# Two transformer blocks on one core: the residual x kept by token instead of by feature, and a rebuilt entry

## The chip, the core and the metric

One Trainium2 chip, one core, no collective. The metric is the device time of one execution in microseconds, median over runs.

## The reference

x is 256 tokens by 1024 features, float32. Two blocks run in sequence:

```python
# block one
h = rms_norm(x, norm_mix_pre)
p = h @ w_in                     # q, k, v, glu, gates
mixed = g_a * (dilated_attention(q, k, v) @ w_attn_out) + g_c * (conv_branch @ conv_pw_w)
x = x + rms_norm(mixed @ w_out, norm_mix_post)
h = rms_norm(x, norm_ffn_pre)
u = causal_depthwise_conv(h @ w_up)
x = x + rms_norm((gelu(u_gate) * u_val) @ w_down, norm_ffn_post)
# block two
x = x + 0.5 * swiglu(rms_norm_2(x, ffn1_norm), w1, w3, w2)
h = rms_norm_2(x, mix_norm)
x = x + (gate_a * rwkv7(h @ w_in) + gate_b * fox(h @ w_in)) @ w_out
x = x + 0.5 * swiglu(rms_norm_2(x, ffn2_norm), w1, w3, w2)
return rms_norm_2(x, final_norm)
```

`rms_norm` divides each token by the root of the mean of its 1024 squares and multiplies by a gain per feature. The squares are summed over features, the gains are per feature.

## The kernel before, in words

All weights stream through three slots of SBUF in chunks of 1 MB (128 x 2048 floats), 172 of them, each loaded by SP's queue once the chunk three before it is split. Splitting makes two fp32r halves of a chunk: `w_hi` by ScalarE (ACT, L1294), `w_lo` by VectorE (DVE, L1551) or, for the first 26 chunks, by GpSimd (POOL, L1244). The activations are split likewise (`X_hi`, `X_lo`, `Y_hi`, `Y_lo`), and each product is three matmuls (`three`, L1918 to L1923).

`by_columns` multiplies 256 output columns of a weight with the whole of X: 16 weight tiles, 3 matmuls of 256 moving columns each, 48 in a chunk. `by_rows` (L1954) takes 256 rows of a weight and adds into all 1024 outputs, again 48 matmuls of 256 columns; its result lies by feature, so x is kept by feature too (`x`, 8 tiles of 128 features by 256 tokens). Only the last feed-forward's down projection is done by tokens: `rows_to_tokens` (L1975) makes the activation the stationary operand and the weight the moving one, 24 matmuls of 512 columns; `x_to_tokens` (L1995) first puts x itself into those banks with 16 fp32 matmuls.

Stages in order, by the index of their first chunk: the entry (chunk 0), the first mixer (glu, qkv, gates, projections, `A_WO` the four chunks of `w_out`, which end at `A_END`), feed-forward 0 (11 rounds of gate, value and down chunk, with a convolution on DVE), feed-forward 1 (to `B0`), the second mixer (to `ffn_at[2]`, its last four chunks from `B_WO` being `w_out_2`), feed-forward 2 and the end. Between two stages lies a boundary:

- The result of the stage lands in four PSUM banks. With a post norm (after `A_END` and feed-forward 0) ACT squares it, PE sums the squares over features with ones (L2009, 4 matmul calls per pair of tiles), ACT takes the root (L1305 loads a table, L1307), DVE makes two diagonals (L1563, L1565), PE spreads them over partitions (L2026), DVE multiplies (L1604) and adds into x (L1609). Without one DVE adds into x directly (L1625).
- ACT makes `X_hi` from x and the gain (L1325), DVE `X_lo` (L1573), and the stage's first chunk is multiplied unnormed as they come.
- For the pre norm ACT squares x (L1300), and after the first chunk PE runs `sum_squares` (L2009, 16 calls, 32 records). The root, the diagonals and the spread follow, the spread in the middle of the second chunk; ACT copies it out as `rstd` (L1316), and every result of the stage is multiplied by it on its way out of PSUM. ACT splits the third chunk between the root and this copy.

The entry: SP loads x (1 MB, one DMA) and chunks 0 to 2. PE turns x by feature (L2074, 16 transposes), DVE copies it out (L1714). ACT's queue issues 16 small loads of parameter rows (L1353); PE turns them at once (L2078), because the first norm's gain is among them. ACT splits chunk 0, then makes `X_hi`. After chunk 0 PE runs `sum_squares`, turns four more groups of parameters (L2095), and makes the table of position biases (L2099), all ahead of chunk 1.

Every order is written out by hand, engine by engine, with counted semaphores. The part of the loop that feeds PE is one `Fori` per feed-forward.

Of the kernel before, what the change touches and what calls it, by code (L numbers as in the profile page):

```python
# [8 lines left out]
F32 = mybir.dt.float32  # L9
# [5 lines left out]
P = 128  # L15
# [73 lines left out]
def block_pair(nc, inp, out, scratch, shifted):  # L89

    ctx = ExitStack()
    with ctx:
# [11 lines left out]
        x = sb("x", [P, NT, T])  # L104
# [3 lines left out]
        eps = sb("eps", [P, 4])  # L108
        rcol, rstd, diag = sb("rcol", [P, 4]), sb("rstd", [P, T]), sb("diag", [P, TT, P])
# [69 lines left out]


# [100 lines left out]
        LAYER_ENDS = (A_WO, A_END, ffn_at[1], B0, ffn_at[2], TOTAL)  # L281
# [21 lines left out]
        x_in = region(0, TT, D)  # L303
        par_in = region(2048, 5, P)

# [4 lines left out]
        final_gain = region(4096, D)  # L310
# [3 lines left out]
        gained = region(6144, 4, 2 * T)  # L314
# [33 lines left out]
        for n in [*range(A_PA), *range(B0, B_RP)]:  # L348
            bank_of[n] = n % 3
            times[n % 3] += 1  # L350
            reads[n] = times[n % 3]

# [68 lines left out]
        def pe_mixer(told, pe, state, by_columns, by_tokens, by_rows, sum_squares, spread):  # L421
            def columns(n, fresh=False, tokens=False, midway=None):
# [36 lines left out]
            columns(B0, fresh=True)  # L459
            sum_squares()  # L460
# [234 lines left out]
            for n in range(B_FP, ffn_at[2]):  # L695
# [4 lines left out]
                else:  # L700
                    r = n - B_WO
                    pe.wait_ge(S["mixed_lo"], 4 + r + 1)
                    by_rows(n, n % RING, 0, X_hi, X_lo, 2 * r, r == 0, r == 3, final=r == 3)


        def act_mixer(told, act, a, split, square, root, spread, state):
# [444 lines left out]
        def _(sp):  # L1151
            told = Count()

            def load(n, slot, parts):

                if n == RING:
                    sp.wait_ge(S["w_lo_first"], 1)
                elif RING < n < BY_POOL + RING:
                    sp.wait_ge(S["w_lo_pool"], n - RING)
# [7 lines left out]
            sp.dma_start(x_in, inp["x"].rearrange("a (t p) d -> p (a t) d", p=P)).then_inc(S["x_landed"], 16)  # L1167
            for n in range(RING):
                load(n, n % RING, chunks[n])
            sp.wait_ge(S["par_cleared"], 1)  # L1170
            for group, row, lo, ap in staged:
                if group > 0:
                    n, c = ap.shape
                    sp.dma_start(par_in[row:row + n, group, lo:lo + c], ap).then_inc(S["rest_landed"], 16)
            sp.dma_start(heads[0:BUCKETS, 0:GROUPS * HPG], inp["rel_bias"]).then_inc(S["rel_landed"], 16)
            gain = inp["final_norm_2"]
            for n in range(RING, TOTAL):
                load(n, n % RING, chunks[n])
                if n == ffn_at[2] + 12:
                    sp.dma_start(final_gain, bass.AP(gain.tensor, gain.offset, [[0, P], [1, D]])).then_inc(  # L1180
                        S["final_gain"], 16)
# [19 lines left out]
        def _(pool):  # L1201
# [19 lines left out]
            g.memset(ones[:], 1.0).then_inc(S["pool_step"], told.one("pool_step"))  # L1221
# [24 lines left out]

# [962 lines left out]
```

## Time and profile before

| what | value |
|---|---|
| median of 3 runs | 1256.07 us (1255.26 to 1256.3) |
| the profiled execution, its own time | 1257.25 us |
| its span, first to last instruction | 1255.5 us |
| mean granted TensorE clock | 0.962 |
| busy: PE, DVE, ACT, POOL | 1197.8, 775.2, 551.0, 154.6 us |
| matmul records on PE | 10503 |
| HBM read, mean rate | 185.70 MB, 150 GB/s |

The span is 1.75 us shorter than that execution's own time, which is 1.18 us above the median. Matmuls overlap in the records, so the step from one start to the next tells the pace, not the duration of one. A granted clock of 1.00 is the full 2.4 GHz, 0.50 is 1.2 GHz.

### The profile page before, as it was taken

The numbers are of one execution on the slowest core, as the hardware profiler recorded it, in microseconds if no ns is written. First come the engines' busy times: TensorE is split into PE (matmuls) and PEld (weight loads), VectorE is DVE, ScalarE is ACT, GpSimd is POOL, SyncE is SP. The second block draws the span as 40 slices with busy tenths as digits, with TensorE's granted clock in tenths as the row PEclk, the third lists the DMA queues.
The fourth block names the chain that finished last, engine by engine and source line by source line (L and its number), as shares of the span: only waits on it lengthen the run. The fifth ranks groups of instructions, "written<-read, shape, count | busy, mean of one in ns | idle before, by whom it ended". The sixth has DMA issues, their size and how long they took to land.

```text
span 1255.5 us, 23871 instructions
## 1 busy us (share of the span) xinstructions
PE 1197.8 (95%) x10503; PEld 1160.5 (92%) x10503; DVE 775.2 (62%) x1057; ACT 551.0 (44%) x613; POOL 154.6 (12%) x113
## 2 busy tenths in 40 slices
PE   6999999989899999989999998999899979999998
PEld 5999999989899999989999997989898879999997
DVE  3588976746587776765554566864266564555554
ACT  4433445473465554453433445523233354444343
POOL 3888770000000000000000000012000000000000
PEclk8999999999799999989999997999999989999999
DMA  6577553345155555526555543332032343565561
GB/s 210 167 233 240 170 168 132 113 146 174 51 184 186 193 175 169 199 65 203 169 169 194 172 151 104 115 103 84 22 101 91 112 134 102 168 210 171 172 199 67
DMA packets 143744, 187.97 MB, mean 150 GB/s; under 512 B 4384, under 2 KB 128857, under 8 KB 143661
## 3 DMA queue, kind: packets, MB, share of 16 engines
q1 hardware_dynamic: 142317, 183.22, 44.5%
q0 software_dynamic: 1104, 3.49, 0.8%
q8 instruction: 63, 1.03, 0.3%
q14 instruction: 20, 0.16, 0.0%
q10 hardware_dynamic: 240, 0.06, 0.0%
HBM read 185.70 MB, written 2.64 MB: 150 GB/s over the span
## 4 chain that ended last, share of the span: by engine, by line
PE 90%; DVE 5%; ACT 3%; issue 1%; ACTq 0%; DMA 0%; POOL 0%; DVEq 0%; POOLq 0%
PE bank L1921 24%; PE bank L1922 24%; PE bank L1923 24%; PE bank L536 2%; PE bank L2009 2%; PE bank L1987 2%; PE bank L1988 2%; PE bank L1989 2%; DVE w_lo L1551 1%; PE bank L596 1%; ACT w_hi L1294 1%; PE bank L2155 1%; DVE bank L1756 1%; PE bank L660 1%; PE bank L662 1%
## 5 line engine op out<-in xcount | busy, mean ns | idle before, releaser
L1921 PE MATMUL bank<-X_hi,w_hi 128*128 128x256 f32 x1968 | 572.3, 291 | 17.2 <-DVE X_lo L1573 11.7
L1922 PE MATMUL bank<-X_lo,w_hi 128*128 128x256 f32 x1968 | 567.3, 288 | 0.0
L1923 PE MATMUL bank<-X_hi,w_lo 128*128 128x256 f32 x1968 | 566.9, 288 | 0.0
L1921 PEld LDWEIGHTS bank<-X_hi,w_hi 128*128 128x128 f32 x1968 | 388.7, 197 | 22.4 <-issue 15.8
L1294 ACT ACTIVATE w_hi<-w_raw 128x2048 fp32r<-128x2048 f32 x172 | 328.5, 1911 | 178.0 <-PE bank L1923 164.8
L1922 PEld LDWEIGHTS bank<-X_lo,w_hi 128*128 128x128 f32 x1968 | 388.8, 198 | 0.4
L1923 PEld LDWEIGHTS bank<-X_hi,w_lo 128*128 128x128 f32 x1968 | 388.4, 197 | 0.0
L1551 DVE TENSOR_TENSOR w_lo<-w_raw,w_hi 128x2048 fp32r<-128x2048 f32 x146 | 333.8, 2287 | 84.1 <-ACT w_hi L1294 83.9
L1654 DVE TENSOR_TENSOR arena<-bank,rstd 128x512 f32<-128x512 f32 x66 | 45.7, 692 | 202.5 <-PE bank L1923 189.8
L1921 PE MATMUL bank<-Y_hi,w_hi 128*128 128x256 f32 x480 | 137.7, 287 | 2.3 <-DVE Y_lo L1103 1.4
L1922 PE MATMUL bank<-Y_lo,w_hi 128*128 128x256 f32 x480 | 136.8, 285 | 0.0
L1923 PE MATMUL bank<-Y_hi,w_lo 128*128 128x256 f32 x480 | 136.7, 285 | 0.0
L1244 POOL TENSOR_TENSOR w_lo<-w_raw,w_hi 128x2048 fp32r<-128x2048 f32 x25 | 116.0, 4647 | 39.3 <-ACT w_hi L1294 39.2
L1921 PEld LDWEIGHTS bank<-Y_hi,w_hi 128*128 128x128 f32 x480 | 93.2, 194 | 3.1 <-DVE Y_lo L1103 1.6
L1756 DVE SCALAR_TENSOR_TENSOR bank<-arena,par,bank 128x256 f32<-128x256 f32 x232 | 93.2, 486 | 0.6
L1922 PEld LDWEIGHTS bank<-Y_lo,w_hi 128*128 128x128 f32 x480 | 93.2, 194 | 0.0
L1923 PEld LDWEIGHTS bank<-Y_hi,w_lo 128*128 128x128 f32 x480 | 93.2, 194 | 0.0
L1275 POOL TENSOR_TENSOR arena<-arena,levels 128x512 f32<-128x512 f32 x10 | 12.7, 1279 | 622.8 <-DVE arena L997 589.2
L1366 ACT ACTIVATE arena<-arena,par 128x256 f32<-128x256 f32 x44 | 24.2, 599 | 71.8 <-DVE arena L1654 71.8
L1375 ACT ACTIVATE arena<-arena 128x512 f32<-128x512 f32 x22 | 14.0, 635 | 88.3 <-DVE arena L1654 88.3
L1589 DVE TENSOR_TENSOR arena<-bank,rstd 128x512 f32<-128x512 f32 x43 | 29.7, 690 | 36.4 <-PE bank L1923 32.4
L1389 ACT ACTIVATE Y_hi<-arena 128x512 fp32r<-128x512 f32 x33 | 20.9, 633 | 44.0 <-DVE arena L1679 25.0
(283 smaller groups left out, 1193.4 us busy)
## 6 DMA issues: line engine op xcount, KB each, us to landing
w_raw<-in_ffn_w_dram SPq DMA_DIRECT2D x66, 1024.0 KB, 5.3
w_raw<-in_w_in_dram SPq DMA_DIRECT2D x54, 1024.0 KB, 5.1
w_raw<-in_w_up_dram SPq DMA_DIRECT2D x22, 1024.0 KB, 5.1
w_raw<-in_w_down_dram SPq DMA_DIRECT2D x11, 1024.0 KB, 4.9
w_raw<-in_w_out_dram SPq DMA_DIRECT2D x8, 1024.0 KB, 4.9
w_raw<-in_conv_pw_w_dram SPq DMA_DIRECT2D x4, 1024.0 KB, 4.8
w_raw<-in_w_attn_out_dram SPq DMA_DIRECT2D x2, 1024.0 KB, 5.0
w_raw<-in_rwkv_proj_dram SPq DMA_DIRECT2D x2, 1024.0 KB, 5.0
```

The lines of the kernel that those rows point to most:

```text
L536: mm = pe.matmul(head(bank[b], h, slice(i * CHUNK, (i + 1) * CHUNK)), left(f, i, h), right(f, i, h), start=True, stop=True)
L1244: g.tensor_tensor(w_lo[n % RING][:, :], raw[n % RING][:, :], w_hi[n % RING][:, :].bitcast(F32), ALU.subtract).then_inc(S["w_lo_pool"], tol ...
L1294: a.activation(w_hi[slot][:, :], raw[slot][:, :], ACT.Copy).then_inc(S["w_hi"], told.one("w_hi"))
L1551: v.tensor_tensor(w_lo[slot][:, :], raw[slot][:, :], w_hi[slot][:, :].bitcast(F32), ALU.subtract).then_inc(S["w_lo"], told.one("w_lo"))
L1589: v.tensor_tensor(dst, pairs(b), over(rstd[:], 2), ALU.mult).then_inc(S[f"bank{b}_read"], 1)
L1654: v.tensor_tensor(u_t[:, side].rearrange("p (m t) -> p m t", m=2), pairs(2 * (i % 2) + side), over(rstd[:], 2), ALU.mult).then_inc(S[name] ...
L1756: v.scalar_tensor_tensor(out=conv[:, t, :] if k == CONV_W - 1 else part, in0=src, scalar=w, in1=part, op0=ALU.mult, op1=ALU.add).then_inc( ...
L1921: pe.matmul(o, wh, xh, start=start, stop=False, skip_group_check=True)
L1922: pe.matmul(o, wh, xl, start=False, stop=False, skip_group_check=True)
L1923: return pe.matmul(o, wl, xh, start=False, stop=stop, skip_group_check=True)
L1987: pe.matmul(o, yh, wh, start=False, stop=False, skip_group_check=True)
L1988: pe.matmul(o, yl, wh, start=False, stop=False, skip_group_check=True)
```

## The change

x lies by token (`x`, two tiles of 128 tokens by 1024 features) from the load to the end. Every down and output projection (`A_WO` to `A_END`, feed-forwards 0 and 1, `B_WO` to `ffn_at[2]`: 30 chunks) goes through `rows_to_tokens`. At each boundary PE turns x into PSUM, 16 transposes, and ACT and DVE make `X_hi` and `X_lo` from there. A token's squares are summed by ACT itself, along the row (`accum_out`), for the post norms and the pre norms; `sum_squares` and `x_to_tokens` go. Gains of post norms are loaded spread over partitions (three DMAs of 512 KB on SP's queue, where there was one). In the entry x and chunk 0 are loaded and split in halves, the first gain is loaded alone and first, ten parameter loads stay on ACT's queue and the rest go to SP's, and all other parameters are turned behind chunk 1 instead of behind chunk 0. Where a stage has no post norm (`B0`, `ffn_at[2]`), the last chunk does the low half of the features first, and PE turns that half two products before the chunk's end, the other half in the middle of the next chunk; with a post norm PE turns all of x after the last chunk, eight transposes for each token tile. `X_hi` is read from PSUM, where a bank's second tile waits for the first one's `X_lo`. The residual of the last feed-forward is added by DVE at the end.

Cut to its core:

```diff
-        x = sb("x", [P, NT, T])
+        x = sb("x", [P, TT, D])
+        HALF_FIRST = (B0, ffn_at[2])
+        TOKEN_ENDS = (A_END, ffn_at[1], B0, ffn_at[2], TOTAL)
 # SP
-            sp.dma_start(x_in, inp["x"]...)
-            for n in range(RING):
+            for h in range(2):
+                sp.dma_start(x[:, :, c], inp["x"]...[:, :, c]).then_inc(S[f"x_landed{h}"], 16)
+            for h in range(2):
+                sp.dma_start(first[:, 4 * h:4 * h + 4, :], chunks[0]...)
+            for n in range(1, RING):
                 load(n, n % RING, chunks[n])
-            for group, row, lo, ap in staged:
-                if group > 0:
+            for group, row, lo, ap in staged[1 + ON_ACT:]:
+            gains = {A_WO: ..., ffn_at[0] + 12: ..., ffn_at[2] + 12: ...}
 # ACT
+            def root_mean(t, halves, root, signal):
+                for h, (source, ready, count) in enumerate(halves):
+                    act.wait_ge(S[ready], count)
+                    a.activation(sq[:, h, :], source, ACT.Square, accum_out=half if h == 0 else whole)
+                    if h == 0:
+                        a.activation(mean, half, ACT.Identity, bias=eps[:, 0:1], scale=1.0 / D)
+                a.activation(root, whole, ACT.Sqrt, bias=mean, scale=1.0 / D)
+            def x_scaled(gain, ends, ahead):
+                for f in range(NT):
+                    high_part(f, gain, ends)
+                for t in range(TT):
+                    token_root(t, ...)
+                split(ahead)
+                spread()
+            act.dma_start(gain_in, inp["norm_mix_pre"]...)
+            for group, row, lo, ap in staged[1:1 + ON_ACT]:
+                act.dma_start(par_in...)
+            root_table()
+            for f in range(NT):
+                if f == 4: first_split(0, "w_hi_first")
+                if f == 6: first_split(1, "w_hi")
+                high_part(f, first_gain, 0)
+            split(1)
+            for t in range(TT): token_root(t, ...)
+            split(2)
+            spread()
 # DVE
+            def post_norm(last, next_gain):
+                for t in range(TT):
+                    for h in range(2):
+                        v.tensor_tensor(gained[:, t, c], bank[4 + 2 * t + h][:, :], token_gain[:, c], ALU.mult)
+                    v.reciprocal(...)
+                    for h in range(2):
+                        v.scalar_tensor_tensor(out=x[:, t, c], in0=gained[:, t, c], scalar=..., in1=x[:, t, c])
+                for f in range(NT): low_part(f, next_gain, last)
+            def residual(last, scale, next_gain, base=4):
+                residual_tile(0, 0); residual_tile(1, 0); low_part(0); low_part(1)
+                residual_tile(0, 1); low_part(2); low_part(3); residual_tile(1, 1)
+                for f in range(4, NT): low_part(f)
 # PE
-                    by_rows(at + 4, ..., 4, Y_hi, Y_lo, ...)
+                    rows_to_tokens(at + 4, ..., (Y_hi, Y_lo), 2 * parity, first and i == 0)
+                    if ends in HALF_FIRST and at == 5:
+                        turn_early_half(ends)
-                sum_squares()
-                x_to_tokens()
+            turn_by_tokens(A_END)
             feed(0)
-                if n == 0:
+                if n == 1:
                     pe.wait_ge(S["constants"], 2)
...
```

## Rows read from the trace of the kernel before

**Rows 1.** the page: busy time of TensorE, and the chain that ended last, by engine
```profile
PE 1197.8 (95%) x10503; PEld 1160.5 (92%) x10503; DVE 775.2 (62%) x1057; ACT 551.0 (44%) x613; POOL 154.6 (12%) x113
...
PE 90%; DVE 5%; ACT 3%; issue 1%; ACTq 0%; DMA 0%; POOL 0%; DVEq 0%; POOLq 0%
```

**Rows 2.** PE's waits over the whole run (total, times, longest, us)
```profile
PE bank L1921 <- DVE X_lo L1573: 11.7, 5, 3.6
...
PE bank L466 <- ACT arena L720: 4.8, 1, 4.8
```

**Rows 3.** PE timeline, one chunk by 256 columns and one by 512
```profile
1097.31 0.28 PE L1921 MATMUL bank<-X_hi,w_hi 128*128 128x256 f32 x1
...
1103.07 0.40 PE L1987 MATMUL bank<-w_hi,Y_hi 128*128 128x512 f32 x1
...
1108.54 0.28 PE L1921 MATMUL bank<-X_hi,w_hi 128*128 128x256 f32 x1
```

**Rows 4.** busy time by stretch: loop, one boundary in four, two later ones
```profile
400.00:417.28 17.28, 17.28 (x147) 17.28 (x146) 12.43 (x16) 8.85 (x10) 0.00 (x0) 1.00 0.56 184
...
319.90:327.30 7.40, 2.46 (x21) 2.19 (x19) 4.88 (x11) 3.74 (x8) 0.00 (x0) 0.78 0.15 61
...
334.70:338.70 4.00, 4.00 (x34) 4.00 (x33) 0.00 (x0) 0.00 (x0) 0.00 (x0) 0.87 0.01 4
...
338.70:344.50 5.80, 5.80 (x28) 5.80 (x29) 0.84 (x4) 2.56 (x3) 0.00 (x0) 0.50 0.00 0
...
344.50:347.60 3.10, 3.10 (x28) 3.10 (x28) 3.10 (x4) 2.50 (x3) 0.00 (x0) 1.00 0.00 0
...
745.40:751.50 6.10, 6.10 (x53) 6.10 (x54) 4.52 (x10) 2.57 (x3) 0.00 (x0) 1.00 0.01 3
...
1071.00:1074.50 3.50, 3.50 (x35) 3.50 (x33) 3.02 (x3) 2.94 (x2) 0.00 (x0) 1.00 0.78 238
```

**Rows 5.** the critical chain in time order: six transposes
```profile
216.81 0.67 PE bank L2131 x6
```

**Rows 6.** DVE timeline, end of the first mixer
```profile
314.43 2.29 DVE L1551 TENSOR_TENSOR w_lo<-w_raw,w_hi 128x2048 fp32r<-128x2048 f32 x1 [3.47 <-ACT w_hi L1294]
...
326.71 0.88 DVE L1573 SCALAR_TENSOR_TENSOR X_lo<-x,par,X_hi 128x256 fp32r<-128x256 f32 x2
```

**Rows 7.** DVE timeline, start of the second mixer
```profile
733.97 1.41 DVE L1625 SCALAR_TENSOR_TENSOR x<-bank,x 128x512 f32<-128x512 f32 x2
...
747.95 2.29 DVE L1551 TENSOR_TENSOR w_lo<-w_raw,w_hi 128x2048 fp32r<-128x2048 f32 x1 [0.80 <-ACT w_hi L1294]
...
750.16 0.68 DVE L1589 TENSOR_TENSOR arena<-bank,rstd 128x512 f32<-128x512 f32 x1
```

**Rows 8.** PE timeline, entry
```profile
5.99 3.65 PE L2074 MATMUL bank<-ident,arena 128*128 128x128 f32 x16 [5.99 <-DMA arena<-in_x_dram]
...
12.34 0.33 PE L2078 MATMUL bank<-ident,arena 128*128 128x128 f32 x1 [2.70 <-DMA arena<-in_rwkv_k_a_dram]
...
15.94 0.55 PE L1921 MATMUL bank<-X_hi,w_hi 128*128 128x256 f32 x1 [3.26 <-DVE X_lo L1573]
...
23.63 3.73 PE L2009 MATMUL bank<-ones,sq 128*128 128x1 f32 x32
...
30.90 0.58 PE L1921 MATMUL bank<-X_hi,w_hi 128*128 128x256 f32 x1
```

**Rows 9.** ACT timeline, entry
```profile
7.34 0.32 ACTq L1353 DMA_DIRECT2D arena<-in_rwkv_k_a_dram  x1
...
9.44 1.91 ACT L1294 ACTIVATE w_hi<-w_raw 128x2048 fp32r<-128x2048 f32 x1 [0.47 <-DMA w_raw<-in_w_in_dram]
```

**Rows 10.** SP timeline, entry
```profile
15.42 43.19 SPq L1165 DMA_DIRECT2D w_raw<-in_w_in_dram  x7
```

**Rows 11.** ACT timeline, last token tile
```profile
1250.01 0.60 ACT L1526 ACTIVATE sq<-bank 128x512 f32<-128x512 f32 x1 [0.34 <-PE bank L1989]
...
1250.73 0.30 ACT L1530 ACTIVATE small<-small 128x1 f32<-128x1 f32 x1
```

More of the change, by code:

```diff
@@ L351, in block_pair, with turned_place @@
             reads[n] = times[n % 3]
+        def turned_place(f, ends):
+            early, late = (2, 3), (4, 5)
+            if ends == B0:
+                early, late = (1, 3), (4, 6)
+            if ends in (0, ffn_at[2]):
+                early, late = (4, 5), (6, 7)
+            c = f % 4 // 2 * T
+            return bank[(early, late)[f // 4][f % 2]][:, c:c + T]
         def all_read(before):
@@ L702, in pe_mixer, with act_mixer @@
                     pe.wait_ge(S["mixed_lo"], 4 + r + 1)
-                    by_rows(n, n % RING, 0, X_hi, X_lo, 2 * r, r == 0, r == 3, final=r == 3)
-        def act_mixer(told, act, a, split, square, root, spread, state):
+                    rows_to_tokens(n, n % RING, (X_hi, X_lo), 2 * r, r == 0, ffn_at[2] if r == 3 else None, base=0)
+        def act_mixer(told, act, a, split, spread, state):
             def copies(ready, count, dst, b, name):
@@ L1952, in by_tokens, with by_rows @@
                 mm.then_inc(S["chunk_used"], told.one("chunk_used"))
[L1954 removed]
+            def by_rows(n, slot, first_bank, hi, lo, k0, first, last, final=False):
                 split_ready(n)
@@ L1984, in rows_to_tokens @@
                     c = k * D + 512 * h
-                    yh, yl = (y[:, k0 + k, t * P:(t + 1) * P] for y in (Y_hi, Y_lo))
+                    yh, yl = (y[:, k0 + k, t * P:(t + 1) * P] for y in (hi, lo))
                     wh, wl = (w[slot][:, c:c + 512] for w in (w_hi, w_lo))
-                    pe.matmul(o, yh, wh, start=False, stop=False, skip_group_check=True)
+                    last = ends is not None and k == 1
+                    pe.matmul(o, yh, wh, start=first and k == 0, stop=False, skip_group_check=True)
@@ L2015, in sum_squares @@
-            def sum_squares():
-                for p in range(4):
-                    sum_pair(p)
+                    mm = pe.matmul(o, yh, wl, start=False, stop=last, skip_group_check=True)
+                    if last and at < 7:
+                        mm.then_inc(S["tile_summed"], told.one("tile_summed"))
+                    if ends in HALF_FIRST and at == 5:
+                        turn_early_half(ends)
+                mm.then_inc(S["chunk_used"], told.one("chunk_used"))
+                if ends is not None:
+                    state["ends"] = ends
```

467 lines of the change are left out of this document (236 added, 231 removed).

## The prediction

> **What bounds the kernel now.** I read the page first. PE is busy for 95% of the span, and it carries 90% of the chain that ended last [rows 1]. So what counts is PE's own work and the few places where it waits. PE's waits add up to little: the largest is five waits for `X_lo`, 11.7 us in all, which are the boundaries between stages, then 4.8 us for the second mixer's first activations [rows 2]. In the loop PE has no gap: 17.28 us for a gate, a value and a down chunk, with DVE busy for 12.43 and ACT for 8.85 [rows 4]. The rest of the loss is seen only by stretches: at a boundary PE counts as busy while it runs small products, or runs at a granted clock of 0.50 [rows 4].
>
> **The down chunks.** A chunk by 256 columns runs from 1097.31 to 1103.07: 48 matmuls, 5.76 us, 120 ns each. The chunk by 512 columns runs from 1103.07 to 1108.54: 24 matmuls, 5.47 us, 228 ns each [rows 3]. Both carry the same 12,288 columns; half as many instructions save 0.29 us. 30 chunks change form. Four of them are the last of a stage and are counted in the boundaries below, so **26 x 0.29 = 7.5 us**. The loop's period falls from 17.28 to 16.99, still above DVE's 12.43 and ACT's 8.85, so all of it is on the path. The Trainium skill (TensorE: Matmul & The Clock Gate, "Back-to-back issue gap") gives a gap of N/2.4 + 2.5 ns, by which the saving of a chunk would be an estimated 24 x 2.5 ns = 0.06 us and this term 1.6 us; the trace disagrees with it in this stream, with 13 ns over the columns' time at 256 and 14 at 512.
>
> **The boundary after the first mixer (`A_END`).** Now: the last chunk starts at 312.2 (PE timeline, 5.76 us and three sums before 319.9). From 319.9 to 327.3 PE mostly waits; the first chunk takes 7.4 us because the clock is low at first; the sums take 4.0; the second chunk takes 5.8 at clock 0.50 and then 3.1 at full clock, to 347.6 [rows 4]. After, from the same start: token tiles end at 313.8, 315.1, 316.5 and 317.8 (6 x 228 ns each). ACT loads its table under the chunk. A square with its accumulator read and the next step takes 0.72, a root 0.30 [rows 11], so ACT has both roots by about 319.9. DVE is the later one: its split ends at 316.7 [rows 6], and then come four products by the gain, two reciprocals and four additions, 0.70 each by the nearest row of that size [rows 7] and 0.15. x's third tile is added at 322.1. PE turns it (16 transposes cost 16 x 0.11 [rows 5] at full clock, twice that at half, of which only two stand ahead of the first `X_hi`), ACT and DVE take 0.45 each [rows 6], and the first chunk starts at **323.8 instead of 327.3**. It still has a gap of 6 us before it, so I leave it 7.4 us. Then the second chunk starts at once, with 48 x 0.12 + 0.4 for the spread = 6.1 us, as in the second mixer's boundary, where no low clock is seen [rows 4]. It ends at 337.4 instead of 347.6: **10.1 us saved**.
>
> What must be ready for the third chunk: ACT ends the last `X_hi` at 326.5, the two roots cost 4 x 0.72 + 4 x 0.30 = 4.1, so 330.6; diagonals 331.4; the spread is due at 333.4, `rstd` 334.4, DVE reads a bank (0.7) and splits (2.29 [rows 6]): 337.3. That is level with PE's 337.4; its cover is gone, and anything later here is time.
>
> **Behind feed-forward 0** the same pattern stands 209 us later, with a last chunk from 521.5 and a first chunk of 7.9 us. DVE is free at 525.7, so by the same steps the first chunk starts at 532.9, the third at 547.0 instead of 556.6: **9.6 us saved**.
>
> **The boundary at `B0`** has no post norm, and no idle to win. Now DVE ends its split at 733.97 and adds two pairs in 1.41 [rows 7]; the last chunk runs from 729.6 to 735.3, the sums from 742.0 to 745.4, the second chunk to 751.5 [rows 4]. After: PE comes to the early transposes at 733.7 and must wait until 735.4 for those two additions; 0.9 for 8 transposes, 1.4 for the rest of the chunk, 1.4 for the first two tiles of the next: 739.1; wait for the last addition until 739.6; 0.9 of transposes; 4.4 for the rest: 744.9. That is only 0.5 earlier than 745.4. What decides is ACT's chain: last `X_hi` at 742.4, roots 4.1, so 746.5 instead of 745.9, then the split of the third chunk, DVE's split (747.95 now) and the read of the bank at 750.16 [rows 7], from which the 4.8 us wait of [rows 2] hangs. **0.5 us lost**, and all that PE gained is waited away.
>
> **The boundary at `ffn_at[2]`** is the same 316.2 us later, but now the second chunk has the low clock and `x_to_tokens` takes 3.5 us to 1074.5 [rows 4]. After: the second chunk runs from 1061.1 to 1067.3; roots at 1062.7, ACT's split to 1064.6, `rstd` 1065.0, bank read 1065.7, split 1067.9. The third chunk starts at 1068.0: **6.5 us saved**.
>
> **The entry.** Now: x landed at 5.99, transposes to 9.6, parameters at 12.34 (the last of 16 issues leaves ACT's queue at 7.66 [rows 9]), chunk 0 starts at 15.94, sums at 23.63, chunk 1 at 30.90, chunk 2 at 38.5 (end of chunk 1) [rows 8]. After: the first half of x lands 1.3 to 1.7 earlier (1 MB takes 3.45, from 5.99 to 9.44 [rows 8, 9]); it is turned at half clock as before, 0.228 each, from 4.7, all of it by 8.4. ACT's eleven issues end at 5.1, its table is loaded by 6.6 with the gain copied; four `X_hi` in turn with DVE to 8.4; half a chunk split to 9.4 (half of 1.91 [rows 9]), its low half on DVE to 10.6. Chunk 0 starts at **10.7 instead of 15.9** and takes 7.7 as now. The second half of chunk 0 lands at 9.44 as now [rows 9] and is split in time (12.8, needed at 15). Chunk 1 starts at 18.4 (its low part is ready at 16.5), takes 6.1, then the parameters take 3.0 (3.5 now, at half clock): chunk 2 at 27.5 instead of 38.5, **11.0 us saved**. ACT's roots end at 18.3, diagonals 19.1, the spread is due at 20.6; POOL has chunk 2 at 24.9. SP's queue takes two halves and five more small loads; it comes to chunk 3 at 15.42 now [rows 10] and some 2 us later then, landed five later, needed at 33. All covered. The first gain takes at most the 5.0 of the last parameter, 7.34 to 12.34 [rows 8, 9]; landing by 5.8 it is still ahead of ACT's 6.6. The two added loads of 512 KB stand in the loop, where DMA's share is 0.56 [rows 4]: no cost.
>
> **The end.** DVE's four additions of 0.70 come between PE and ACT; two of them do not fit beside 1.37 per tile together with the products by the gain: **1.4 us lost** (0.7 if they fitted).
>
> **Sum:** 7.5 + 10.1 + 9.6 - 0.5 + 6.5 + 11.0 - 1.4 = 42.8 us. 1257.25 - 42.8 = 1214.45 for the profiled execution; the median lies 1.2 lower: **1213.3 us**.
>
> **The rivals.**
> - *The clock (0.15).* The transposes and the stalls of 1.7 us could let the clock fall where it now stays up: chunk 2 of the entry behind 3.0 us of parameters, and the chunks at `ffn_at[2]`. A fall cost 5.8 us at 0.50 where 2.7 fewer would do [rows 4]; twice that and 1 us at two others is 6 to 7: 1220. Against it: 3.4 us of sums at 742 did not lower it. The Trainium skill (TensorE: Matmul & The Clock Gate, "PE-mode transpose") says that transposes do not count as busy for the clock; it would give this time. No run here shows it yet: the entry's transposes ran at half clock, from a cold start.
> - *The new chain (0.2).* Roots, spread, bank read and split end later than I have them and gate the third chunk at each of four places by about 2 us: 1221. For it: there is no slack left in three of them. ACT now does eight serial steps where it had four squares.
> - *The gap between the two forms is not there in the loop (0.05).* 7.5 us less: 1221.
> - *Faster still (0.1).* The clock is up for the first chunks, or the first gain and x come sooner: 3 + 3 + 2 less: 1205.
> - *The entry doesn't deliver (0.06).* Small loads queue behind x and chunk 0, or ACT's issues take longer: half of 11.0 is lost: 1219.
> - *Slower (0.02).* The down chunk's operands come late in the loop: ACT and DVE work for `f_lo` is in series, and with the shorter period PE waits in every round. It decides only if each of 22 rounds waits over 2.1 us (46 us in all); then 1259. DVE's 4.85 free microseconds of 17.28 speak against it.
>
> **How the numbers follow.** Forecast 0.42, rivals as given. From 1204 (faster still) to 1225 (two of the lesser ones together) lies 0.8; I leave out the slow end. A measurement tells this kernel from no change at about 0.2%, 2.5 us; all cases but the last lie far beyond: faster 0.96, same 0.02, slower 0.02.
>
> **What would show it.** No L2009 rows; 720 fewer records of main matmuls; the down chunks at 228 ns; chunk 0 at about 10.7 and chunk 2 at 27.5; at both post norms a gap of some 6 us before the first chunk with small waits; at `B0` two waits of 1.7 and 0.5 inside the chunks and the 4.8 us wait grown by about 1; at the end the last square 0.7 later behind the last matmul. I am wrong if a third chunk waits for `w_lo`, if a clock of 0.50 stands in the second chunks, or if the loop's period is not 17.0.

## The result and the profile after

The changed kernel takes **1211.9 us** (median of 4 runs, 1211.0 to 1214.9), the kernel before 1255.7 (1254.9 to 1256.3): a ratio of **0.9656, interval 0.9638 to 0.9674**. The forecast was 1213.3, in a range from 1204 to 1225. The profiled execution took 1212.24 us with a span of 1210.5, against a span of 1255.5 before: 45.0 us to explain, where the working had 42.8.

The page of the changed kernel, the lines of busy time and of the chain that answer to [rows 1]:

```profile
PE 1155.8 (95%) x9584; PEld 1086.6 (90%) x9584; DVE 770.4 (64%) x1042; ACT 557.2 (46%) x660; POOL 149.9 (12%) x112
...
PE 87%; DVE 7%; ACT 4%; issue 2%; DMA 0%; ACTq 0%; DVEq 0%
```

PE has the same share in a shorter span: what went was time in which it counted as busy (one-column products, half clock, more instructions), as the stretches of [rows 4] had hinted. PE's waits, to set beside [rows 2] (total, times, longest, us; L735 is the line that was L720, and L2042 turns x):

```profile
PE bank L481 <- ACT arena L735: 5.6, 1, 5.6
PE bank L2042 <- DVE x L1660: 4.9, 4, 1.4
PE bank L2224 <- ACT arena L1529: 4.5, 4, 3.6
PE bank L2042 <- DVE x L1676: 3.5, 4, 1.5
PE bank L2097 <- DVE X_lo L1159: 3.5, 1, 3.5
```

The five waits for `X_lo` at the stage boundaries are gone. In their place stand eight short ones for x itself, 4.9 and 3.5 us; the wait behind `B0` is the largest now, 5.6 where it was 4.8.

The down chunk by 512 columns, in the PE timeline of the loop of feed-forward 0 (start, duration of one), as the second chunk of [rows 3]:

```profile
337.54 0.40 PE L2097 MATMUL bank<-w_hi,Y_hi 128*128 128x512 f32 x1
...
343.00 0.28 PE L1987 MATMUL bank<-X_hi,w_hi 128*128 128x256 f32 x1
...
354.52 0.40 PE L2097 MATMUL bank<-w_hi,Y_hi 128*128 128x512 f32 x1
```

It takes 5.46 us, and the loop's period is 354.52 - 337.54 = 16.98, as forecast (17.28 before).

The entry, in the PE timeline, beside [rows 8]:

```profile
2.38 0.24 PE L2146 MATMUL bank<-ident,arena 8*128 8x8 f32 x1 [2.38 <-DMA arena<-in_norm_mix_pre_dram]
4.97 3.37 PE L2042 MATMUL bank<-ident,x 128*128 128x128 f32 x16 [2.35 <-DMA x<-in_x_dram]
11.06 0.36 PE L1987 MATMUL bank<-X_hi,w_hi 128*128 128x256 f32 x1 [2.71 <-issue]
...
24.59 0.27 PE L2163 MATMUL bank<-ident,arena 128*128 128x128 f32 x1
...
25.22 1.45 PE L2168 MATMUL bank<-arena 32*4 32x256 f32 x6
26.61 0.39 PE L1987 MATMUL bank<-X_hi,w_hi 128*128 128x256 f32 x1
```

Chunk 0 starts at 11.06 (15.94 before), chunk 2 at 26.61 (38.48 before, the end of chunk 1).

Stretches of the changed kernel (us, busy time and instructions of PE, PE's weight loads, DVE, ACT and POOL, then the granted clock, 1.00 being the level of 2.4 GHz and 0.50 that of 1.2 GHz; a value between is a mixture):

```profile
281.10:283.50 2.40, 0.09 (x2) 0.05 (x1) 2.27 (x5) 1.30 (x3) 0.00 (x0) 1.00 0.88 291
283.50:288.00 4.50, 4.50 (x13) 3.53 (x14) 3.39 (x3) 1.76 (x1) 0.00 (x0) 0.62 0.22 78
306.70:312.80 6.10, 3.34 (x18) 1.99 (x18) 5.46 (x11) 3.16 (x12) 0.00 (x0) 0.91 0.51 172
312.80:315.20 2.40, 2.40 (x12) 2.40 (x12) 1.98 (x6) 2.12 (x6) 0.00 (x0) 0.52 0.00 0
315.20:325.70 10.50, 10.50 (x90) 10.50 (x89) 4.21 (x7) 8.30 (x18) 0.00 (x0) 1.00 0.00 0
...
718.20:723.80 5.60, 5.60 (x17) 4.19 (x17) 3.79 (x4) 3.20 (x5) 0.00 (x0) 0.50 0.08 15
724.00:728.20 4.20, 4.20 (x21) 4.20 (x22) 1.37 (x3) 3.20 (x5) 0.00 (x0) 0.51 0.64 222
```

The boundary at `A_END`: a gap of 6.1 us with two turns in it, 2.4 us of the first chunk at half clock, and then 10.5 us at full clock through the rest of the first and all of the second chunk, where before stood 5.8 us at 0.50 [rows 4]. Each stretch behind a long wait of PE (from 283.5, 312.8 and 718.2) shows a low clock.

**Where the 45.0 us came from**, each piece taken between the same two starts of chunks on PE in both traces (the third chunk of a stage is the end of a boundary and the start of what follows):

| piece | before | after | gain | forecast |
|---|---|---|---|---|
| entry, to the start of chunk 2 | 38.48 | 26.61 | 11.9 | 11.0 |
| first mixer, to `A_END`'s last chunk | 273.7 | 274.9 | -1.2 | 0.9 |
| boundary at `A_END` | 35.3 | 24.4 | 10.9 | 10.1 |
| loop of feed-forward 0 | 173.9 | 171.2 | 2.7 | 2.9 |
| boundary behind feed-forward 0 | 35.2 | 23.8 | 11.4 | 9.6 |
| loop of feed-forward 1 | 173.0 | 170.0 | 3.0 | 2.9 |
| `B0`, to the end of the wait for ACT | 27.2 | 27.2 | 0.0 | -0.5 |
| second mixer | 289.1 | 287.4 | 1.7 | 0.9 |
| boundary at `ffn_at[2]` | 28.7 | 21.7 | 7.1 | 6.5 |
| the end | | | -2.3 | -1.4 |

### The profile page after: what moved, and what is told of

The parts are those of the page before. It is cut to its first block, busy times and chain, and to the rows that moved or that the text cites. A ratio compares the mean times of both kernels' runs of the same rounds, so it can differ in the third digit from the quotient of the medians.

```text
span 1210.5 us, 22075 instructions
## 1 busy us (share of the span) xinstructions
PE 1155.8 (95%) x9584; PEld 1086.6 (90%) x9584; DVE 770.4 (64%) x1042; ACT 557.2 (46%) x660; POOL 149.9 (12%) x112
## 4 chain that ended last, share of the span: by engine, by line
PE 87%; DVE 7%; ACT 4%; issue 2%; DMA 0%; ACTq 0%; DVEq 0%
PE bank L1987 20%; PE bank L1988 20%; PE bank L1989 19%; PE bank L2097 5%; PE bank L2098 5%; PE bank L2099 5%; PE bank L551 2%; DVE w_lo L1602 2%; ACT w_hi L1316 1%; PE bank L611 1%; PE bank L2042 1%; PE bank L2224 1%; DVE bank L1819 1%; PE bank L675 1%; PE bank L677 1%
## 5 line engine op out<-in xcount | busy, mean ns | idle before, releaser
L1987 PE MATMUL bank<-X_hi,w_hi 128*128 128x256 f32 x1840 | 529.2, 288 | 2.8 <-issue 2.7
L1988 PE MATMUL bank<-X_lo,w_hi 128*128 128x256 f32 x1840 | 525.5, 286 | 0.0
L1989 PE MATMUL bank<-X_hi,w_lo 128*128 128x256 f32 x1840 | 525.2, 285 | 0.0
L1988 PEld LDWEIGHTS bank<-X_lo,w_hi 128*128 128x128 f32 x1840 | 358.1, 195 | 1.2
L2097 PE MATMUL bank<-w_hi,Y_hi 128*128 128x512 f32 x264 | 103.3, 391 | 1.2 <-DVE Y_lo L1742 1.2
L2098 PE MATMUL bank<-w_hi,Y_lo 128*128 128x512 f32 x264 | 103.1, 390 | 0.0
L2099 PE MATMUL bank<-w_lo,Y_hi 128*128 128x512 f32 x264 | 102.7, 389 | 0.0
L2097 PEld LDWEIGHTS bank<-w_hi,Y_hi 128*128 128x128 f32 x264 | 49.7, 188 | 11.1 <-DVE Y_lo L1742 1.6
L2099 PEld LDWEIGHTS bank<-w_lo,Y_hi 128*128 128x128 f32 x264 | 49.6, 188 | 10.6
L2098 PEld LDWEIGHTS bank<-w_hi,Y_lo 128*128 128x128 f32 x264 | 49.7, 188 | 9.1
```

Source lines behind the costliest of these rows:

```text
L1987: pe.matmul(o, wh, xh, start=start, stop=False, skip_group_check=True)
L1988: pe.matmul(o, wh, xl, start=False, stop=False, skip_group_check=True)
L1989: return pe.matmul(o, wl, xh, start=False, stop=stop, skip_group_check=True)
L2097: pe.matmul(o, yh, wh, start=first and k == 0, stop=False, skip_group_check=True)
L2098: pe.matmul(o, yl, wh, start=False, stop=False, skip_group_check=True)
L2099: mm = pe.matmul(o, yh, wl, start=False, stop=last, skip_group_check=True)
```

## The experiments

Theory: the gain is PE time, in three kinds. Half as many matmuls in the down chunks; one-column products, the turn back to tokens and idle time taken out of the boundaries; and, as a consequence that I had counted only in part, less time at half clock. Rivals: the 512-column form gains nothing where other engines hide it; the third chunk of a stage waits for the row scale anyway, so that what stood ahead of it cost little; the entry's gain has one source alone. Medians in different series differ by up to 3.5 us for one kernel (1254.3 and 1257.8 for the kernel before), so each edit is read at its place in the trace first and in the median second.

### Half width

```diff
-                    pe.matmul(o, yl, wh, start=False, stop=False, skip_group_check=True)
+                    for q in range(2):
+                        c2 = slice(256 * q, 256 * q + 256)
...
+                        pe.matmul(o[:, c2], yl, wh[:, c2], start=False, stop=False, skip_group_check=True)
...
```

> Edit: every 512-column matmul of the down, A_WO and B_WO chunks is issued as two of 256 columns, nothing else. Theory (a matmul costs its columns plus some 13 ns): 41 chunks x 0.29 us = 11.9 us more than the changed kernel's 1211.9, so 1223.8, and each such chunk again near 5.76 us. Rival (a back-to-back matmul costs its columns plus 2.5 ns): 41 x 0.06 = 2.5 us, so 1214.4. Rival (the 256-column form is hidden behind the other engines in the loops): under 4 us, so below 1216.

Measured 1223.5 us (1220.7 to 1225.6), ratio 0.9728 (0.9702 to 0.9754); the span is 1221.7, 11.2 longer than the changed kernel's. The same place in its PE timeline:

```profile
337.23 0.28 PE L2099 MATMUL bank<-w_hi,Y_hi 128*128 128x256 f32 x1
...
343.11 0.28 PE L1988 MATMUL bank<-X_lo,w_hi 128*128 128x256 f32 x1
```

49 matmuls in 5.88 us, 120 ns each, against 24 in 5.46 above. The width of the instruction is worth 0.3 us a chunk. For the kernel it is worth 9 us by the ratios (0.9728 - 0.9656, of 1256) and 11.2 by the spans, where 11.9 was expected; both rivals (2.5, and under 4) fall, so little of it is hidden. A matmul of this stream costs 13 to 14 ns over its columns' time at either width. The Trainium skill (TensorE: Matmul & The Clock Gate, "Back-to-back issue gap") has 2.5 ns there for a matmul by itself, from which an estimated 1214.4 would have followed; for a stream of weight loads and matmuls the same section has about 131 ns at 512 columns, against the 228 ns seen here. The measurement decides against both.

### Sums back, and turns in their place

```diff
                 mm.then_inc(S["chunk_used"], told.one("chunk_used"))
                 if fresh:
                     state["xg"] += 1
+                    for i in range(16):
+                        pe.matmul(bank[3][:, 256 + i % 2:257 + i % 2], ident[:], ident[:, 0:1], start=True, stop=True)
```

The second kernel has `for i in range(32): pe.transpose(bank[3][:, 256:384], ident[:], ident[:])` there instead.

> Edit: behind the first chunk of each of the five fed stages 16 fp32 matmuls of one column, as the kernel before had for its sums of squares, with no wait of their own and no reader. Theory (their time stood in the way in four of five places, and the clock fell behind them): some 3.5 us at the entry, A_END, ffn_at[1] and ffn_at[2] = 14, little at B0, where 5.6 us of idle time follow, and up to 2.9 us more in each place where the granted clock falls to half behind them: 1226 to 1235. Rival (the third chunk waits for the row scale anyway, so they are absorbed): 0 to 5 us more, 1212 to 1217.

> Edit: in the same five places 32 fp32 transposes of 128x128 instead (0.11 us each at full clock, 3.5 us together). Theory from the traces (transposes at full length hold the clock, as 16 of them did between two chunks at B0): 4 x 3.5 = 14 us more, 1226, and a granted clock of 1.00 in the chunk behind them at B0 and ffn_at[2]. Rival (transposes do not count as work for the clock, which the Trainium skill's page TensorE: Matmul & The Clock Gate states under PE-mode transpose; what follows from it is that the chunk behind them is at half clock for some microseconds): 2.9 us more in up to five places, 1229 to 1240, and a granted clock near 0.5 there.

With the sums 1236.8 us (1234.9 to 1239.3), ratio 0.9830 (0.9808 to 0.9853), span 27.0 longer; with the turns 1228.0 (1223.1 to 1232.0), ratio 0.9752 (0.9719 to 0.9786), span 19.8 longer. (By the ratios it is 21.9 and 12.1 us; the profiled execution of the turns was the slowest of its four.) Both groups last 3.5 us. Stretches of the kernel with the sums: the sums of feed-forward 1's boundary, then what follows:

```profile
525.70:529.30 3.60, 3.60 (x35) 3.60 (x33) 0.00 (x0) 0.83 (x1) 0.00 (x0) 0.99 0.00 0
529.30:532.60 3.30, 3.30 (x17) 3.30 (x17) 0.00 (x0) 0.00 (x0) 0.00 (x0) 0.50 0.00 0
```

The same two of the kernel with the turns:

```profile
521.60:525.10 3.50, 3.50 (x35) 3.50 (x33) 0.65 (x3) 2.15 (x3) 0.00 (x0) 1.00 0.00 0
525.10:529.00 3.90, 3.90 (x35) 3.90 (x34) 0.58 (x1) 0.38 (x1) 0.00 (x0) 1.00 0.00 0
```

Of the five places, the clock fell behind the sums in three (entry, feed-forward 1, `ffn_at[2]`), behind the turns in none; in the kernel before it fell behind the sums in four of five, which is the low second chunk of [rows 4]. Some 37 matmuls ran slow behind the sums, at 0.09 us more each: about half of the 7.2 us between the two spans. A good part of the rest stands in chunks ahead of the sums (the first chunks of the entry and of feed-forward 1 had 26 and 19 slow matmuls in the one trace, 16 and 4 in the other), and the same chunks differ as much between two executions of one kernel (26 and 19 in `after_again`, 15 and 5 in the first execution). So the rival that I gave 0.15, that the new transposes lower the clock, is not borne out. The rule beside it, in the Trainium skill (TensorE: Matmul & The Clock Gate, "PE-mode transpose"), was that a transpose doesn't count as busy for the clock; these fp32 turns, which the trace lists as matmuls of 107 ns, held 1.00 for 3.5 us and in the 4 us behind. Whether they use the mode that the page means, no run here shows.

The price at the place: with the turns the third chunk starts 3.5 us later at the entry, `A_END`, feed-forward 1 and `ffn_at[2]`, the full length, so there the row scale doesn't gate it; behind `B0` only 1.2, because the wait for ACT falls from 5.6 to 3.5. That leaves 19.8 - 4 x 3.5 - 1.2 = 4.6 us, and they stand in the second mixer, whose code is the same. I come back to them.

### The entry, part by part

```diff
 entry_whole:
-            for h in range(2):
-                c = slice(512 * h, 512 * (h + 1))
-                sp.dma_start(x[:, :, c], inp["x"].rearrange("a (t p) d -> p (a t) d", p=P)[:, :, c]).then_inc(
-                    S[f"x_landed{h}"], 16)
+            sp.dma_start(x[:, :, :], inp["x"].rearrange("a (t p) d -> p (a t) d", p=P)).then_inc(S["x_landed0"], 16)
...
 params_early:
-                if n == 1:
+                if n == 0:
                     pe.wait_ge(S["constants"], 2)
...
 gain_last:
-            act.dma_start(gain_in, inp["norm_mix_pre"][0].rearrange("(r c) -> r c", c=P)).then_inc(S["par_landed"], 16)
             act.wait_ge(S["par_cleared"], 1)
             for group, row, lo, ap in staged[1:1 + ON_ACT]:
...
+            act.dma_start(gain_in, inp["norm_mix_pre"][0].rearrange("(r c) -> r c", c=P)).then_inc(S["par_landed"], 16)
```

> Edit: x and the first chunk are loaded in one transfer each instead of in halves; the instructions behind them are the same. Theory (the halves let transposes and splits start while the second half is under way, a part of the entry's 11.9 us): the first chunk starts 1 to 2 us later, 1213 to 1214. Rival (the entry is set by the chain of splits, not by landing): within 0.4 us of 1211.9. Rival (two transfers less on the queue help): down to 1211.

> Edit: the parameters are turned behind the first chunk again (as before the change), and copied by DVE behind its first bank; the rest of the entry stays changed. Theory (what matters of this part is only that the last parameter lands near 18.3 us, when the first chunk ends): PE waits under 1 us behind the first chunk and the third chunk starts 0 to 1.5 us later than 26.6 us. Rival (behind the first chunk the eleven small products let the clock fall, as in the kernel before): the second chunk runs at half clock for a while, 2 to 3 us in all. Rival (the position is worth the whole 3.7 us that it took before): 3 us or more.

> Edit: the transfer of the first norm weight is issued behind the ten other parameter transfers of ACT's queue instead of ahead of them. Theory (the entry hangs on x, turned at 4.97 us, and on the ACT table load to 6.6 us; the weight is needed from then on): it is issued near 5.0 us, lands near 7 us, and the first chunk starts 0.5 to 1.5 us later than 11.06 us. Rival (the weight alone is the part that the entry's gain comes from): 3 us or more. Rival (it is hidden behind the first splits): under 0.3 us.

`entry_whole`, 1215.6 us (1215.2 to 1216.4), ratio 0.9669 (0.9649 to 0.9689). Its PE timeline:

```profile
6.17 3.68 PE L2035 MATMUL bank<-ident,x 128*128 128x128 f32 x16 [3.56 <-DMA x<-in_x_dram]
12.04 0.55 PE L1980 MATMUL bank<-X_hi,w_hi 128*128 128x256 f32 x1 [2.19 <-issue]
```

x comes 1.2 us later and chunk 0 0.98 later; with 27 slow matmuls behind it instead of 15 the third chunk starts at 28.81, 2.2 later. The halves are worth 1 us, the low end of the theory; the rest is clock, which `after_again` also has, with its halves (26 slow matmuls).

`params_early`, 1215.5 us (1213.1 to 1218.0), ratio 0.9678 (0.9650 to 0.9707). Its PE timeline behind chunk 0, and the stretch of chunk 1:

```profile
20.24 0.30 PE L2163 MATMUL bank<-ident,arena 128*128 128x128 f32 x1 [1.81 <-DMA arena<-in_conv_dw_w_dram]
20.38 0.60 PE L2165 MATMUL bank<-ident,arena 128*128 128x128 f32 x4
20.91 2.22 PE L2168 MATMUL bank<-arena 32*4 32x256 f32 x6
```

```profile
23.00:27.10 4.10, 4.10 (x20) 4.04 (x20) 0.00 (x0) 0.00 (x0) 2.15 (x1) 0.50 0.43 127
```

Here I was wrong by the size: the last parameter lands at 20.24, not 18.3, so PE waits 1.81; turns and products take 2.8 us instead of 2.0; and the second chunk, 17 of its matmuls at half clock, takes 8.6 instead of 6.2. All that follows starts 5.0 us later. Two of the rivals together are right: having the parameters behind the second chunk is worth 5 us, some 3 of it clock.

`gain_last`, 1217.5 us (1215.8 to 1218.2), ratio 0.9690 (0.9666 to 0.9714). Its issues on ACT's queue, then its PE timeline:

```profile
5.61 0.32 ACTq L1395 DMA_DIRECT2D arena<-in_norm_mix_pre_dram  x1
5.96 1.28 ACT L1354 ACT_TABLE_LOAD   x1 [5.96 <-issue]
```

```profile
10.88 0.24 PE L2146 MATMUL bank<-ident,arena 8*128 8x8 f32 x1 [10.88 <-DMA arena<-in_norm_mix_pre_dram]
11.06 3.67 PE L2042 MATMUL bank<-ident,x 128*128 128x128 f32 x16
16.93 0.55 PE L1987 MATMUL bank<-X_hi,w_hi 128*128 128x256 f32 x1 [2.20 <-issue]
```

I expected 0.5 to 1.5 us and got 5.9: the first chunk starts at 16.93. The 4 KB are issued at 5.61 and landed at 10.88, 5.3 us, behind x and the first megabytes of weights; in the changed kernel they are the first issue of the queue, at 0.81, and have landed by 2.38, in at most 1.6 us. What makes it so dear is PE's order: the gain's own transpose (L2146) stands ahead of those of x (L2042), so x, there since 4.75 and 6.45, is turned only from 11.06, and ACT, its table loaded at 7.24, waits 4.82 us for it. Of the three parts tried, this one delays the third chunk most: 5.9 us, against 5.0 and 2.2. Whether x turned first would have hidden it, no run shows.

### The orders of ACT and DVE around B0

```diff
 squares_early:
                 for f in range(NT):
                     high_part(f, gain, ends)
+                    if f == 3 and ends in HALF_FIRST:
+                        for t in range(TT):
+                            half_mean(t, first + t + 1)
...
 update_first:
                 residual_tile(last, scale, 0, 0, base)
                 residual_tile(last, scale, 1, 0, base)
+                split(last + 1)
                 low_part(0, next_gain, last)
```

(In `update_first` the split is taken out ahead of the stage's end in exchange.)

> Edit: at B0 and ffn_at[2] ACT squares the two early halves of x between the fourth and the fifth high part, where it waits 2.2 us for late transposes, instead of behind the eighth. Theory (at B0 the chain late high parts, four squares, root, split, scale, bank read sets the 5.58 us that PE waits for ACT L735; two squares and a mean less stand in it): the wait shrinks by 1.5 to 2 us, nothing at ffn_at[2]: 1.5 to 2 us less in all. Rival (that wait is set by the bank reads of DVE and its split, so it moves little): under 0.5 us. Rival (the squares delay the fifth high part and with it the first chunk): 0.5 us more.

> Edit: at B0 and ffn_at[2] DVE adds the two early tiles to x ahead of its last split, not behind it, so that PE's transposes in the last chunk don't wait 1.51 us. Theory: 1.5 us less at ffn_at[2], and 1.5 us less at B0 since the high parts and roots all come earlier: 3 us in all. Rival (the split then delays the low parts, so that the first chunk waits as much): 0 to 1 us in all. Rival (B0's gain vanishes in the wait for ACT L735): 1.5 us.

`squares_early`, 1216.2 us (1214.1 to 1217.8), ratio 0.9679 (0.9652 to 0.9705). In its waits of PE:

```profile
PE bank L481 <- ACT arena L735: 3.6, 1, 3.6
```

5.6 became 3.6, so ACT's serial roots do set that wait: the chain that I named for `B0` is shown. The median shows nothing of it, though: the second mixer's stretch behind it (to the end of PE's wait for DVE L1066) takes 181.8 us, where it took 178.8, and up to PE's wait for `X_lo` at `B_WO` it takes 273.0, where it took 265.7.

`update_first`, 1213.1 us (1210.8 to 1216.3), ratio 0.9667 (0.9641 to 0.9694). DVE's timeline in the last chunk ahead of `B0`:

```profile
690.59 0.69 DVE L1676 SCALAR_TENSOR_TENSOR x<-bank,x 128x512 f32<-128x512 f32 x1 [1.33 <-PE bank L2101]
691.95 0.69 DVE L1676 SCALAR_TENSOR_TENSOR x<-bank,x 128x512 f32<-128x512 f32 x1 [0.67 <-PE bank L2101]
692.55 2.28 DVE L1602 TENSOR_TENSOR w_lo<-w_raw,w_hi 128x2048 fp32r<-128x2048 f32 x1
```

Both tiles are added before the split, and PE's two waits of 1.51 us are gone. Counted from the third chunk of feed-forward 1, the wait for ACT ends 1.3 us earlier (195.96 instead of 197.22 us behind it), and `ffn_at[2]`'s third chunk starts 1.3 earlier, counted from PE's wait for `X_lo` at `B_WO`: 2.6 where 3 was expected. (From the third chunk of feed-forward 0 the first of the two looks like 2.1, but 0.9 of that is the boundary behind feed-forward 0, where the clock fell for no matmul in this trace and for five in the other.) The span is only 1.4 shorter, since the mixer between took 2.9 back.

### The same kernel again, and PE kept busy

```diff
+            def keep_busy(n, b, count):
+
+                split_ready(n)
+                for _ in range(count):
+                    pe.matmul(bank[b][:, :], w_hi[n % RING][:, 0:P], w_hi[n % RING][:, 0:512], start=True, stop=True)
...
             columns(B0 + 1, midway=spread)
+            keep_busy(B0 + 2, 6, 22)
...
+                        pe.wait_ge(S["attn_gated"], 4)
+                        keep_busy(n, 7, 9)
                     pe.wait_ge(S["mixed_lo"], r + 1)
```

and the like at the other places (at the entry ten fp32 matmuls of 128 columns). The tail's edit in `order_all` is DVE's order alone:

```diff
+            residual_tile(TOTAL, 0.5, 0, 0)
+            residual_tile(TOTAL, 0.5, 0, 1)
             for t in range(TT):
                 for h in range(2):
-                    residual_tile(TOTAL, 0.5, t, h)
+                    if t == 1 and h == 0:
+                        residual_tile(TOTAL, 0.5, 1, 1)
...
+                if t == 0:
+                    residual_tile(TOTAL, 0.5, 1, 0)
```

> Edit: none, the changed kernel once more, beside the three below. It gives the spread of its stages between executions. Theory (the second mixer, from the end of its wait for ACT L735 to the wait for DVE L1066, took 178.8 to 182.1 us in nine kernels that are the same there, by where the clock falls): total 1211 to 1216, that stretch anywhere from 178.8 to 182.1. Rival (the longer stretches come from the edits made in the experiments): 178.8 again.

> Edit: three orders at once. The two early tiles ahead of DVE's last split (update_first), the early squares between the fourth and fifth high part (squares_early), and in the tail the additions of the last tiles ahead of the gains and of the reciprocal of the tile before. Theory: 2.1 at B0 and 1.3 at ffn_at[2] as measured alone, 2.0 more at B0 for the squares, about 1 us in the tail from the last matmul to the end (7.8 us in the changed kernel): 6 us less, less what falls of the clock take back in the second mixer. Rival (the mixer takes it back by the clock): the total is within 2 us of after_again though the three places are shorter.

> Edit: only matmuls that nobody reads, in places where PE waits: behind the turns at the entry (10 fp32 of 128 columns), at A_WO (9 of 512 columns), in the three gaps of each of A_END and ffn_at[1] (5 or 2, 6 and 2), ahead of the wait for lora_act behind B0 (22) and at B_WO (7). Theory (the granted clock falls behind an idle PE): the slow matmuls behind these gaps (15, 9, 9, 5, 19 and 8 in the changed kernel) go to full pace: 48 x 0.12 + 17 x 0.18 = 8.8 us less; where some gaps are overfilled, 5 to 9 us less. Rival (the clock falls there whatever PE does in the gap): no slow matmul less, and 0 to 3 us more from overfilled gaps. Rival (the falls move to other places): within 2 us of after_again.

> Edit: order_all and keep_warm together, with 14 instead of 22 matmuls behind B0, where the gap is shorter. Theory: the gains of both add, 10 to 14 us less than after_again, 1198 to 1203. Rival (the clock takes it back): 1206 to 1210.

All four beside the same runs of the kernel before:

| kernel | median (range), us | ratio (interval) |
|---|---|---|
| `after_again` | 1214.7 (1211.2 to 1217.7) | 0.9654 (0.9637 to 0.9671) |
| `order_all` | 1207.1 (1205.1 to 1211.9) | 0.9595 (0.9582 to 0.9608) |
| `keep_warm` | 1203.5 (1203.3 to 1207.2) | 0.9570 (0.9557 to 0.9583) |
| `order_warm` | 1198.6 (1197.2 to 1200.0) | 0.9527 (0.9514 to 0.9540) |

`after_again` has the ratio of the first measurement. Its mixer took 181.7 us between the two waits where the first execution took 178.8, and 270.3 where it took 265.7 up to the wait for `X_lo`, from the same code: so the 3 to 5 us that the second mixer took back in `turns_there` and `update_first` need be no effect of the edits. The 273.0 of `squares_early` lie 2.7 above that; `order_all`, with the same edit, has 270.7. A part of it at half clock, in `after_again`:

```profile
725.00:730.50 5.50, 5.50 (x28) 5.50 (x28) 2.54 (x2) 2.98 (x5) 0.00 (x0) 0.50 0.47 164
```

`keep_warm`, the stretches behind the gaps, to set beside those of the changed kernel above (283.5, 312.8, 718.2 and 724.0):

```profile
283.60:288.00 4.40, 4.39 (x19) 3.67 (x20) 3.24 (x3) 1.82 (x2) 0.00 (x0) 1.00 0.27 95
311.30:315.30 4.00, 4.00 (x34) 3.97 (x34) 2.84 (x7) 3.65 (x10) 0.00 (x0) 1.00 0.00 0
505.50:509.70 4.20, 4.20 (x36) 4.20 (x36) 2.80 (x7) 3.85 (x10) 0.00 (x0) 1.00 0.00 0
709.10:714.80 5.70, 5.17 (x24) 3.94 (x22) 2.61 (x6) 3.92 (x6) 0.00 (x0) 1.00 0.59 184
714.80:717.80 3.00, 2.96 (x17) 2.40 (x17) 1.20 (x1) 2.66 (x4) 0.00 (x0) 1.00 0.00 0
717.80:722.00 4.20, 4.20 (x35) 4.20 (x36) 3.49 (x6) 3.87 (x7) 0.00 (x0) 1.00 0.44 127
```

None of these is below 1.00. The slow matmuls behind the gaps that the expectation counts are gone, and so is one thing that it didn't: the 16 products behind `B0`'s wait take 3.0 us instead of 5.6. So at these six places the clock fell behind a waiting PE, and work that nobody reads kept it up. The gain is 10.5 us by the ratios (0.9654 - 0.9570, of 1256), a little more than the 5 to 9 expected, and the slowest of its five executions is faster than the fastest of `after_again`'s. But the expected sum doesn't come out of it place by place: a slow matmul costs 0.21 instead of 0.12 us, not twice as much, so that the 48 are worth 4.5 us. In the two profiled executions the gain is 10.5 as well (1216.0 and 1205.5): 2.3 at the entry, nothing (-0.3) to the third chunk behind `A_END`, 2.2 to that of feed-forward 1, 4.7 in the second mixer (2.6 of it the 16 products), 1.6 at `B_WO`. Against the first execution of the changed kernel it is only 5.0, for the second mixer took 265.7 us there without filling and 265.6 here with it: the clock falls again further on, here from 733 on:

```profile
733.20:743.20 10.00, 10.00 (x31) 6.75 (x31) 6.97 (x9) 5.01 (x7) 0.00 (x0) 0.50 0.49 147
```

So the rival that the falls move is true in part. And part of the filling overshoots: at `A_WO` the first chunk starts at 283.61, where 282.5 was due by the earlier entry.

`order_all` gains 7.4 us by the ratios, where 6 were expected; its rival, within 2 us, falls. The tail from the first addition to the end takes 1210.0 - 1199.10 = 10.9 us instead of 1210.5 - 1198.75 = 11.75. It starts in DVE's timeline with:

```profile
1199.10 0.69 DVE L1702 SCALAR_TENSOR_TENSOR x<-bank,x 128x512 f32<-128x512 f32 x1 [4.02 <-PE bank L2132]
```

`order_warm` has both, 15.9 us, more than the 10 to 14 expected. It beats both kernels, the one before by 59 us (0.0473 of 1256) and the changed one by 16. With 14 instead of 22 matmuls behind `B0` its 16 products still run at full clock, but the chunk behind them doesn't:

```profile
708.70:711.50 2.80, 2.80 (x16) 2.22 (x16) 1.09 (x1) 2.46 (x4) 0.00 (x0) 1.00 0.00 0
711.90:715.00 3.10, 3.10 (x16) 3.10 (x16) 2.97 (x5) 3.10 (x6) 0.00 (x0) 0.50 0.35 87
```

## Why the prediction was right

The sum was 42.8 and the profiled executions differ by 45.0; no term was off by more than 2.1 us, and the likeliest case came true. That the median came out within 1.4 us is partly luck: the errors of the terms have both signs, and the changed kernel itself had medians of 1211.9 and 1214.7 in two series.

- **The down chunks**: right, 120 and 228 ns again, 5.46 us a chunk, and `half_width` gives 9 to 11 us back, for 41 chunks. Taken as 20 chunks in the loops, 5.7 of 5.8. The rest of the 7.5 stood in the mixers and can't be told from their clock.
- **`A_END`**: "the first chunk starts at 323.8 instead of 327.3", 11.6 us behind the start of the last chunk; it was 11.3. "It still has a gap of 6 us before it, so I leave it 7.4": it took 6.8, with 2.3 us at half clock. The second chunk at full clock, the third behind it without a wait: right. 10.9 instead of 10.1.
- **Behind feed-forward 0**, 11.4 instead of 9.6: the step that failed is "a first chunk of 7.9 us". It took 6.5 us, for the clock was back after 1.4. In `after_again` 19 matmuls were slow in that chunk instead of 5, and it took 7.8: the term was right for one execution in two.
- **`B0`**: no gain, as said; roots of 4.1 us right, 703.36 to 707.43. The wait grew from 4.8 to 5.6 (forecast "by about 1"). `squares_early` shows ACT's chain to be the cause.
- **`ffn_at[2]`**: 7.1 instead of 6.5.
- **The entry**: chunk 0 at 11.06 (10.7), the parameters 2.0 us instead of 3.0 because the clock stayed up. "The first gain takes at most the 5.0 of the last parameter ... landing by 5.8": it landed at 2.38, and `gain_last` shows what it would have cost otherwise.
- **The end**: -2.3 instead of -1.4, and the last square starts 1.9 us later behind the last matmul, not 0.7. The term took two additions. DVE's timeline shows what stood with them ahead of the second token tile and was left out, the wait for the first tile's root, the reciprocal and the scaling:

```profile
1201.95 0.17 DVE L1961 RECIPROCAL stat<-stat 128x1 f32<-128x1 f32 x1 [0.45 <-ACT stat L1337]
1202.15 0.49 DVE L1966 TENSOR_SCALAR arena<-arena,stat 128x512 f32<-128x512 f32 x1
1202.55 0.68 DVE L1676 SCALAR_TENSOR_TENSOR x<-bank,x 128x512 f32<-128x512 f32 x1
```

  `order_all`, which moves an addition ahead of them, gives 0.85 back.
- **The first mixer**: 0.9 of wide chunks were counted and 1.2 were lost. At `A_WO` PE waits 2.3 us, 2.0 before, and then nine matmuls of 512 columns run at 1.2 GHz, 405 ns each instead of 228: 1.6 us. `half_width` waits there as long and shows no slow matmul, `keep_warm` doesn't either; so it is the clock. Whether the wider form has a part in it stays open: `entry_whole`, `params_early` and `after_again` have the wide form and no slow matmul there. At `B_WO` seven to eleven wide matmuls ran slow in nine of the ten traces of the wide form without filling, and in the narrow form, before and in `half_width`, 16 narrow ones each, which costs as much (1.5 us).
- **The rivals**: the new chain (0.2) is out, since whatever is put ahead of the third chunk delays it in full at four of five places. The clock (0.15) is out in the form that I gave it: no fall stood behind the transposes at `B0` and `ffn_at[2]`, behind those added in `turns_there`, or in a second chunk. The gap between the forms (0.05) is out. None of the three signs of being wrong showed: no third chunk waits for `w_lo`, no second chunk has the low clock, the period is 16.98. "Faster still" named the right sign of what was left: the clock was better than forecast.

The step behind the small miss is one for all: I carried low-clock time over from the boundaries of before. Matmuls of 256 columns in slow groups (five or more in a row, 0.20 to 0.22 us from start to start) number 233 in the trace before and 116 in the one after; at 0.09 us more each, that is some 11 us of the 45. Against it stand the chunks at `A_WO` and `B_WO`, whose wide matmuls lost 3.5 us to the clock (7.2 us each instead of 5.44). And how much of the rest is the change and how much the execution, two traces can't tell: `after_again` has 166.

## What to carry to other kernels

Count instructions of a PE-bound loop as well as columns, and look at what keeps PE "busy": in this kernel one-column products, and products behind a wait, were where the time was. The small transfer that the start hangs on belongs at the head of its queue: issued eleventh instead of first, it landed 8.5 us later. Where PE must wait some microseconds, matmuls that nobody reads can keep what follows at full clock, if they end before the wait does; here, in six places, that gave 10.5 us against one execution of the changed kernel and 5.0 against another.

## What the runs showed of the hardware

- The granted clock's falls differ between executions of the same instructions. The second mixer's stretch took 178.8 to 182.1 us in twelve traces of kernels without filling matmuls (before included, 179.8), and 178.8 and 181.7 in two of one kernel; with the gap ahead of it filled, 175.9 twice, of which the 16 products explain 2.6. Up to the wait for `X_lo` at `B_WO` two executions of one kernel took 265.7 and 270.3, so differences below some 5 us need the local reading.
- One-column fp32 products (16 in 3.5 us) were followed by half clock in 3 of 5 places (in 4 of 5 in the kernel before), 32 full turns of the same length in none of 5. Each is one trace.
- 4 KB took 5.3 us from issue to landing with weights under way, at most 1.6 as the first transfer of its queue.
